# U blocks of the expert layer beside the gates: one 512-column product for the high weights, the halves added on VectorE, the chosen experts turned 6 blocks sooner

## What is computed

```python
def peer_ffn(xn, w_peer_q, sub_keys, expert_u, expert_v):
    ...
    s = jnp.einsum('thpd,hpnd->thpn', qh, sub_keys).astype(jnp.float32)
    sv, si = lax.top_k(s, PEER_TOPK)
    cand = (sv[:, :, 0, :, None] + sv[:, :, 1, None, :]).reshape(...)
    best, pick = lax.top_k(cand, PEER_TOPK)
    expert_idx = jnp.take_along_axis(cand_idx, pick, axis=-1)
    gates = jax.nn.softmax(best, axis=-1)
    ...
        u = expert_u[ic]
        hval = jnp.einsum('cd,chkd->chk', xc, u).astype(jnp.float32)
        a = (gc * jax.nn.gelu(hval, approximate=False)).astype(xc.dtype)
        return jnp.einsum('chk,chkd->cd', a, expert_v[ic])
```

## Time and profile before

| | before |
|---|---|
| median of 3 runs | 1405.58 us (1405.32 to 1405.79) |
| the profiled execution | 1404.01 us |
| its span | 1402.2 us |
| TensorE busy, matmuls | 1388.1 us (99%), 8604 matmuls |
| VectorE busy | 987.7 us (70%) |
| ScalarE busy | 809.0 us (58%) |
| mean granted TensorE clock | 0.999 |

### The profile page before, as it was taken

The page is one execution under the profiler, slowest core; times in us unless marked ns, Lnnn a source line. Parts: engine busy times, 40 slices in busy tenths (PEclk is TensorE's granted clock), DMA queues, the critical chain, the costliest instruction groups (busy, mean ns, idle before and its releaser), DMA issues.

```text
span 1402.2 us, 22369 instructions
## 1 busy us (share of the span) xinstructions
PE 1388.1 (99%) x8604; PEld 1244.6 (89%) x8604; DVE 987.7 (70%) x1790; ACT 809.0 (58%) x1533; POOL 41.8 (3%) x49
## 2 busy tenths in 40 slices
PE   8999999999999999999999999999999999999998
PEld 6998888888898888899999999999988888888886
DVE  7877766666786567789997777778766555555555
ACT  6875555554665554554445877776655444555543
POOL 3002030000000000000000000000000000000000
PEclk9999999999999999999999999999999999999999
DMA  6533476665454446545556444444456656555562
GB/s 228 181 121 128 135 217 191 180 191 185 159 159 135 149 153 235 184 151 183 170 175 208 139 150 136 136 146 141 147 165 217 224 194 195 195 194 193 191 193 100
DMA packets 67568, 240.95 MB, mean 172 GB/s; under 512 B 8453, under 2 KB 8837, under 8 KB 67078
## 3 DMA queue, kind: packets, MB, share of 16 engines
q1 hardware_dynamic: 67462, 239.52, 52.8%
HBM read 237.39 MB, written 2.10 MB: 171 GB/s over the span
## 4 chain that ended last, share of the span: by engine, by line
PE 87%; DVE 8%; ACT 2%; issue 1%; DMA 0%; POOL 0%; SPq 0%; POOLq 0%; ACTq 0%; DVEq 0%
PE bank L2131 85%; DVE wl L542 3%; PE bank L2229 1%; PE bank L2217 1%; ACT wh L1527 1%; DVE eq L1370 1%; DVE eq L1373 1%; DVE ij L1376 1%; DVE St L732 0%; ACT kdz L1533 0%; DMA x<-in_x 0%; DVE pos__227 L1307 0%; DVE h L567 0%; DVE x L1041 0%; DVE sgt L1039 0%
## 5 line engine op out<-in xcount | busy, mean ns | idle before, releaser
L542 DVE TENSOR_TENSOR wl<-raw,wh 128x1024 fp32r<-128x1024 f32 x429 | 523.2, 1226 | 263.8 <-ACT wh L1527 262.8
L2131 PE MATMUL bank<-hTb,wh 128*128 128x256 f32 (+2 forms) x2864 | 596.4, 302 | 0.9 <-DVE wl L542 0.9
L1527 ACT ACTIVATE wh<-raw 128x1024 fp32r<-128x1024 f32 x429 | 448.6, 1054 | 232.4 <-PE bank L2131 229.3
L2131 PEld LDWEIGHTS bank<-hTb,wh 128*128 128x128 f32 (+1 forms) x2864 | 456.5, 191 | 17.2 <-issue 1.4
L2131 PE MATMUL bank<-hTb,wl 128*128 128x256 f32 (+1 forms) x1640 | 454.3, 282 | 0.0
L2131 PE MATMUL bank<-wh,hTb 128*128 128x512 f32 x1488 | 426.3, 393 | 1.2 <-DVE hTb L576 0.8
L2131 PEld LDWEIGHTS bank<-wh,hTb 128*128 128x128 f32 x1488 | 279.7, 188 | 60.1 <-DVE wl L542 1.5
L2131 PEld LDWEIGHTS bank<-hTb,wl 128*128 128x128 f32 (+1 forms) x1640 | 312.3, 190 | 4.5
L2131 PE MATMUL bank<-wl,hTb 128*128 128x512 f32 x744 | 244.9, 390 | 0.0
L2131 PEld LDWEIGHTS bank<-wl,hTb 128*128 128x128 f32 x744 | 140.2, 189 | 28.2
L2054 ACT ACTIVATE gates<-bank 128x256 f32<-128x256 f32 (+31 forms) x118 | 38.1, 323 | 76.7 <-PE bank L2131 76.6
(11 more groups left out here) (384 smaller groups left out, 1170.9 us busy)
## 6 DMA issues: line engine op xcount, KB each, us to landing
raw<-in_wts SPq DMA_DIRECT2D x441, 512.0 KB, 3.3
x<-in_x SPq DMA_DIRECT2D x4, 256.0 KB, 4.8
sk<-in_sk SPq DMA_DIRECT2D x1, 1024.0 KB, 6.7
spill<-x SPq DMA_DIRECT2D x1, 1024.0 KB, 7.7
x<-spill SPq DMA_DIRECT2D x1, 1024.0 KB, 6.2
out<-h SPq DMA_DIRECT2D x4, 256.0 KB, 2.1
gb<-in_g_ffn SPq DMA_DIRECT2D x1, 512.0 KB, 4.6
gb<-in_norm_mix_g SPq DMA_DIRECT2D x1, 512.0 KB
```

The lines of the kernel that those rows point to most:

```text
L542: e.tensor_tensor(b[:, :], raw[u % RAW][:, :], a[:, :].bitcast(F), ALU.subtract).then_inc(S("lo"), 1)
L1527: e.activation(parts_of(u)[0][:, :], raw[u % RAW][:, :], ACT.Copy).then_inc(S("hi"), 1)
L2131: return e.matmul(o, l, r, start=first, stop=last, skip_group_check=True)
```

## The change

- `NP` goes from 53 to 47. The turning of the choice, and all that follows, comes 6 blocks sooner: blocks 48 to 111 lie beside the gates, 112 to 127 behind them.
- Every block after NP has the form `unit_M`, also the 64 beside the gates.
- ScalarE gets `block_out(n)`: it waits for block n, copies the second half of its bank to a new tile `us` (two of them in turn), and only then splits the next unit. Gelu reads `us`, after the one-hots of that turn, and waits for `u_sum`.
- VectorE gets `summed(n)` at the head of each turn: it waits for that copy and adds the first half of the bank to it. The unit that it splits right behind is n+2, not n+3 as before.
- `ga` has 4 tiles instead of 5.
- In the blocks behind the gates the copy now comes before the split of the next unit, and not behind it, on ScalarE; the sum comes before the split on VectorE.

```diff
-NP, NB = 53, 5
+NP, NB = 47, 5
...
-        ga = [M(f"ga{i}", [128, 256]) for i in range(5)]
+        ga = [M(f"ga{i}", [128, 256]) for i in range(4)]
+        us = [sb("us0", [128, 256], F, X0 + 5120), M("us1", [128, 256])]
...
+            def summed(n):
+
+                u = us[n % 2][:, :]
+                e.wait_ge(S("u_out"), n - NP)
+                e.tensor_tensor(u, B[2 + n % 4][:, 0:256], u, ALU.add).then_inc(S("u_sum"), 1)
 
             low(nth("U", ORDER[NP]) + 2)
             for c in range(NB - 1):
                 one_hots(c)
-            low(nth("U", ORDER[NP]) + LOOK)
             for c in range(64):
                 n = NP + 1 + c
-                low(nth("U", ORDER[n]) + LOOK)
+                summed(n)
+                low(nth("U", ORDER[n]) + 2)
                 if c + NB - 1 < 64:
                     one_hots(c + NB - 1)
                 gated(n)
...
             for n in range(NP + 65, NE - 2):
-                low(nth("U", ORDER[n]) + LOOK)
                 summed(n)
+                low(nth("U", ORDER[n]) + 2)
                 gated(n)
...
             def gelu(n):
                 c, b = built(n), B[2 + n % 4]
                 high(nth("U", ORDER[n]) + LOOK)
-                e.wait_ge(S("done"), nth("U", ORDER[n]) + 1)
+                if n <= NP:
+                    e.wait_ge(S("done"), nth("U", ORDER[n]) + 1)
+                else:
+                    e.wait_ge(S("u_sum"), n - NP)
+                    b = us[n % 2]
                 if c:
-                    if n >= NP + 7:
-                        e.wait_ge(S("gated_2"), n - NP - 6)
-                    if c == 256:
-                        copy(ga[n % 5][:, :], b[:, 256:512]).then_inc(S("late"), 1)
-                        e.wait_ge(S("late_sum"), n - NP - 64)
-                    t = e.activation(ga[n % 5][:, 0:c], (ga[n % 5] if c == 256 else b)[:, 0:c], ACT.Gelu)
+                    if n >= NP + 6:
+                        e.wait_ge(S("gated_2"), n - NP - 5)
+                    t = e.activation(ga[n % 4][:, 0:c], b[:, 0:c], ACT.Gelu)
...
+            def block_out(n):
+
+                e.wait_ge(S("done"), nth("U", ORDER[n]) + 1)
+                copy(us[n % 2][:, :], B[2 + n % 4][:, 256:512]).then_inc(S("u_out"), 1)
+                high(nth("U", ORDER[n]) + LOOK)
...
             for c in range(64):
                 n = NP + 1 + c
-                gelu(n)
+                block_out(n)
                 if c + NB - 1 < 64:
                     one_hots(c + NB - 1)
+                gelu(n)
...
-                if built(n) == 256:
+                if n > NP:
                     unit_M(("U", ORDER[n]), B[2 + n % 4])
```

More of the change, by code:

```diff
@@ L1442, in gated @@
                     e.wait_ge(S("gelu"), n + 1)
-                    e.tensor_tensor(g[:, 0:c], g[:, 0:c], ga[n % 5][:, 0:c], ALU.mult).then_inc(S("gated_2"), 1)
+                    e.tensor_tensor(g[:, 0:c], g[:, 0:c], ga[n % 4][:, 0:c], ALU.mult).then_inc(S("gated_2"), 1)
+            def summed(n):
+                u = us[n % 2][:, :]
+                e.wait_ge(S("u_out"), n - NP)
+                e.tensor_tensor(u, B[2 + n % 4][:, 0:256], u, ALU.add).then_inc(S("u_sum"), 1)
             low(nth("U", ORDER[NP]) + 2)
@@ L2119, in scalar @@
                 if n in (1, 2):
+                    block_out(NE - 3 + n)
                     gelu(NE - 3 + n)
```

## The result

| | before | changed |
|---|---|---|
| median | 1405.32 us (5 runs, 1404.21 to 1405.79) | 1398.47 us (5 runs, 1397.84 to 1398.71) |
| the profiled execution | 1404.01 us | 1398.65 us |
| its span | 1402.2 us | 1396.9 us |
| TensorE busy, matmuls | 1388.1 us, 8604 | 1382.7 us, 8044 |
| VectorE busy | 987.7 us | 1009.0 us |

The account below looks back on a forecast made before the run. TensorE's own work was taken as the bound. Savings of 4.1 us (form) and 0.4 (move) made 4.5, so 1404.01 became 1399.5; plus 1.57 of median offset, 1401.1 us. Range 1399.0 to 1404.2.

Parts of the forecast that it names:

- What bounds the kernel: From the choice on only TensorE's own work counts; it is busy 99% of the span.
- What the new form saves: On TensorE, 64 blocks beside the gates save 0.064 us each, 4.1 us; with 0.09 each, 5.8.
- The move by six blocks: Six more blocks behind NP get the short form: 6 x 0.064 = 0.4 us saved.
- What has to stay hidden: ScalarE's copy and VectorE's sum in 64 turns cost nothing; split 1.9 to 1.8 us ahead, some 1.3 by the end.
- The start: Choice turned at 757.3; unit 50 split by 767.1, TensorE wants it at 768.1: narrowest place, 1.0 us.
- Behind the gates: TensorE does not wait in the 16 blocks there; nothing gained beyond the form.
- The range: 1399.0 (6.5 us off) to 1404.2 (the small saving), around a forecast carrying over 1.57 us of median above profiled execution.
- the whole 0.09 comes through: Rival: each block saves the 0.09 seen right behind gates, 6.2 us in all, 1399.4; within the forecast's own range.
- cheap-columns rival: A matmul costs its columns and little else; beside the gates only 0.02 a block saved, 1.4 us, 1404.2; chance 12%.
- late split: Rival: copy, sum and split exceed their spare time, TensorE waits for VectorE; 8.3 us more, 1413.5; chance 5%.

Follow-up runs that it names:

- late_small: Changed kernel with four small float32 products of 128 columns, result unused, put behind each of the 16 blocks behind the gates: 1411.86 us.
- late_round: Changed kernel with two unused fp32r products of 256 columns behind each of the 16 blocks behind the gates, none behind the last: 1400.90 us.
- np47_old: Kernel before with only NP moved from 53 to 47, old form beside the gates and old order behind them: 1404.44 us, ratio 0.9999.
- sum_x2: Changed kernel with one extra unused sum of 256 columns on VectorE in each of the 64 turns beside the gates: 1398.83 us.
- sum_x3: Changed kernel with two extra unused VectorE sums in each of the 64 turns, each followed by a wait for its end: 1423.47 us.
- late_one: Changed kernel with one small float32 product of 128 columns, result unused, behind each of the 16 blocks behind the gates: 1401.19 us.
- in_turn: Changed kernel with each 512-column product followed by its 256-column one to the end, in all short-form blocks: 1400.16 us, ratio to before 0.9968.
- parted: Changed kernel with 512-column products first, then the 256-column ones, in 42 gate and up weight blocks and 16 behind the gates: 1397.33 us, ratio to before 0.9947.

## Why the prediction was wrong

The sign and the mechanism were right, the size was not: 1401.1 forecast, 1398.47 measured, 0.5 us below the range. The miss of 2.6 us has two parts: 1.7 in the saving (6.2 for 4.5) and 0.9 in the base that it was taken from.

- *What bounds the kernel*: right. TensorE bounds the stage, and no new wait came.
- *What the new form saves*: **this term of the sum was mis-sized.** I had two rows, 0.064 us from eight blocks in a row behind the gates and 0.09 from the one block behind gates, and took the first because more blocks stood behind it. Measured: 0.094 a turn, 64 x 0.094 = 6.0 us instead of 4.1. The one block was the nearest row: it alone had the same work ahead of it as the 64 to come. `late_small` and `late_round` show that what stands ahead of a block is what parts the two figures. I gave the single block no weight in the forecast, only in the range. The other row also said less than I read from it: the difference does not hold in every one of the eight blocks. With the start of the next block in before,

```profile
1024.47 0.63 PE L2131 MATMUL bank<-hTb,wh 128*128 128x512 f32 x2
```

  the first of the eight, from 1021.68 on, takes 2.79 us, and the other seven 2.82. The pace was still fast in the second block behind the gates and slow from the third on, which could be seen beforehand.
- *The move by six blocks*, 0.4 us: right, 0.35 in `np47_old`. The choice was turned 0.9 us later than forecast (758.17 against 757.3), because the whole program ran 0.9 us late before it.
- *What has to stay hidden*: right that it costs nothing, and right in its leads: 1.9 to 1.6 us forecast as 1.9 and 1.8, and 1.25 at the end, forecast as 1.3. VectorE's room was underrated. The whole durations that I added up count overlaps twice: the sum takes 0.33 and not 0.42. `sum_x2` shows that another 0.33 us a turn would have been free, if barely.
- *The start*: right in time, but it is not the narrowest place. VectorE's timeline there has

```profile
766.30 0.42 DVE L1450 TENSOR_TENSOR us<-bank,us 128x256 f32<-128x256 f32 x1 [1.75 <-ACT us L1534]
766.64 1.22 DVE L543 TENSOR_TENSOR wl<-raw,wh 128x1024 fp32r<-128x1024 f32 x1
```

  so unit 50 is split by 767.9, where 767.1 and the 0.9 of lateness make 768.0, and TensorE takes it at 769.0, 1.1 us later, without a wait; 1.0 was forecast.
- *Behind the gates*: right that TensorE does not wait, but this is where the new order is narrowest, and I worked out no lead for it. There a block is not followed by 0.81 us of gates, and the chain copy, sum, split starts at the end of each block. VectorE's split and TensorE's start of the block that needs it (the second product of the row):

```profile
1009.02 1.22 DVE L543 TENSOR_TENSOR wl<-raw,wh 128x1024 fp32r<-128x1024 f32 x1
...
1010.65 0.63 PE L2142 MATMUL bank<-hTb,wh 128*128 128x512 f32 x2
```

  The split ends at 1010.24, the block starts at 1010.89: 0.65 us ahead, the same in 14 of the 16 blocks. Before, in the old order, the lead there was 8.6 us at the first block and 3.3 at the last. VectorE idles 0.93 us a block in this stage, so what is short is the chain and not its load.
- *The range* **is the second step that failed.** I added to the sum the 1.57 us by which the median of three runs of before, 1405.58, lay above its profiled execution. The changed kernel has no such offset: its median is 0.2 us below its profiled execution. And 1405.58 was a high median; the four larger sets of before gave 1404.40 to 1405.32. Less the 6.2 of the traces, 1405.58 gives 1399.4, inside the range; the other 0.9 us to 1398.47 are the spread of executions. Their first 40 us alone differ by 1.5: the 200th matmul starts between 40.22 and 41.69 us in the 13 traces. My range reached 0.3 us beyond the largest saving I had worked out and left no place for that.
- *Rivals*: "the whole 0.09 comes through" is what happened. The cheap-columns rival is refuted: 0.094 us a turn came, not 0.02. Its figure of 262 cycles for 256 columns (the Trainium skill, "TensorE: Matmul & The Clock Gate", section "Back-to-back issue gap") does not hold for these products either: they take 0.120 us each, where 262 cycles at 2.4 GHz come to an estimated 0.109. The late split did not come, though `sum_x3` shows it is real.

What stays open: why a pair costs 0.353 us in a row of such blocks and 0.346 behind certain other products. Ruled out are the stage and its traffic (`late_one` beside `late_round`), the neighbours at the seam (`in_turn`), and the need for float32 products ahead (`late_round`). Nor are gate products ahead enough in every order of the block (`in_turn`, every third turn).

## What to carry to other kernels

Where two rows price the same edit, take the one with the same neighbours on the engine, even if it stands alone. Between two orders of the same matmuls there was up to 1% of a block here (2.79 us against 2.82, turns of 3.673 against 3.700), and the better order beside the gates was the worse one behind them: with no wait anywhere, measure them. An engine's room is worked out from distances of starts; whole durations understate it. And a new wait chain is worked out for every stage that it runs in: here the stage that looked safe had the least lead.

And put the spread of executions into the range on its own: a third of the miss here (0.9 of 2.6 us) had no mechanism in it.

## What was not expected of the hardware

- An fp32r matmul of this kernel takes its columns at 2.4 GHz (granted clock 1.00 in these stretches) plus about 13.3 ns, in rows of equal ones: 0.120 us for 256 columns (0.1067), 0.2267 for 512 (0.2133), the former in the stage of the choice, the latter in the D stage, where before has six products in 1.36 us:

```profile
1053.62 1.07 PE L2131 MATMUL bank<-wh,hTb 128*128 128x512 f32 x4
...
1054.98 1.07 PE L2131 MATMUL bank<-wh,hTb 128*128 128x512 f32 x4
```

  A pair would then take 0.347 us, which is the fast pace; the slow one is 0.006 us above it. Eight products fewer would save 0.107 us a block; beside the gates 0.094 of it came, in a row 0.064.
- The remainder depends on the sequence ahead, in cycles that repeat from block to block to within a few ns. In `parted` the eight 512-column products behind a row of 256-column ones take 0.028 us more in all than 8 x 0.2267, and the first 256-column one behind them 0.007 less than 0.120: 2.79 us a block, where the figures above give 2.773.
- VectorE at 100% busy over 30 us (`sum_x2`) delayed nobody, as long as its lead, 0.44 us at the least, lasted.
